# The last expert round taken out of the loop of a mixture-of-experts step, its rows added by a weighted one-hot matmul in PSUM

## What is computed

```python
for g in range(N_GROUPS):                       # 4 groups of 8 experts, top-2 of the best group
    h1 = jnp.einsum('td,edf->tef', xt, exp_w1[g])    # 1024 -> 256
    h3 = jnp.einsum('td,edf->tef', xt, exp_w3[g])
    act = jax.nn.silu(h1) * h3 * comb[:, g, :, None]
    out = out + jnp.einsum('tef,efd->td', act, exp_w2[g])
return x + out.reshape(n, t, D_MODEL)
...
y = rms_norm(x, final_norm_g)
```

## Time and profile before

| | |
|---|---|
| median of 3 runs | 716.58 us (715.87 to 720.83) |
| the profiled execution | 718.26 us, its span 716.3 us |
| PE busy / weight loads | 618.3 us / 451.2 us |
| DVE, ACT, POOL busy | 319.0, 201.5, 79.2 us |
| DMA | 179.38 MB, mean 250 GB/s |
| mean granted clock of PE | 0.931 |

### The profile page before, as it was taken

One profiled execution on the slowest core, in us unless ns is written; L12 is line 12 of the kernel. 1 busy time (PEld: TensorE's weight loads), 2 busy tenths in 40 slices (PEclk: granted clock), 3 DMA queues, 4 the chain that ended last, 5 costly groups with the idle time before them and its releaser, 6 DMA issues.

```text
span 716.3 us, 11504 instructions
## 1 busy us (share of the span) xinstructions
PE 618.3 (86%) x4673; PEld 451.2 (63%) x4673; DVE 319.0 (45%) x629; ACT 201.5 (28%) x343; POOL 79.2 (11%) x129
## 2 busy tenths in 40 slices
PE   4999999989899999999989985999999798398720
PEld 3999998579899999984778862333333343033200
DVE  4748978958544364688413155121121121012038
ACT  5512332254743434436003051121121121012022
POOL 0000000510001210010202111111212111110100
PEclk8999999999999999999989985999999999699965
DMA  9941220324556233669896394899999999999453
GB/s 284 279 141 64 96 82 2 121 79 125 168 129 214 81 118 119 234 239 342 277 389 254 150 350 181 337 420 420 418 421 421 418 422 419 422 420 402 190 233 136
DMA packets 74924, 179.38 MB, mean 250 GB/s; under 512 B 9166, under 2 KB 55946, under 8 KB 61544
## 3 DMA queue, kind: packets, MB, share of 16 engines
q1 hardware_dynamic: 65900, 163.47, 60.9%
q0 software_dynamic: 5600, 12.76, 4.7%
q10 hardware_dynamic: 3372, 2.42, 1.0%
HBM read 172.80 MB, written 15.61 MB: 263 GB/s over the span
## 4 chain that ended last, share of the span: by engine, by line
PE 68%; DMA 17%; DVE 6%; SPq 4%; issue 3%; ACT 2%; ACTq 1%; DVEq 0%; POOLq 0%
DMA w<-exp_w 13%; PE ps L1678 12%; PE ps L1680 12%; PE ps L1679 12%; PE ps L2121 11%; PE ps L2149 4%; PE ps L1827 3%; SPq L612 3%; PE ps L1674 3%; PE ps L1908 2%; DMA raw<-cache_mem_k 2%; DMA xs_rows<-x_sample 1%; PE ps L2008 1%; PE ps L1845 1%; PE ps L1970 1%
## 5 line engine op out<-in xcount | busy, mean ns | idle before, releaser
L2121 PE MATMUL ps<-w,xeT 128*64 128x512 f32 (+2 forms) x512 | 122.9, 652 | 22.9 <-DMA w<-exp_w 21.6
L1678 PE MATMUL ps<-xH,w_h 128*128 128x260 f32 x480 | 139.0, 290 | 0.4 <-DVE xL L1336 0.2
L1679 PE MATMUL ps<-xH,w_l 128*128 128x260 f32 x480 | 136.2, 284 | 0.0
L1680 PE MATMUL ps<-xL,w_h 128*128 128x260 f32 x480 | 136.2, 284 | 0.0
L2121 PEld LDWEIGHTS ps<-w,xeT 128*64 128x64 f32 (+2 forms) x512 | 42.2, 147 | 102.0 <-issue 100.2
L1678 PEld LDWEIGHTS ps<-xH,w_h 128*128 128x128 f32 x480 | 91.1, 190 | 5.6 <-issue 4.9
L1679 PEld LDWEIGHTS ps<-xH,w_l 128*128 128x128 f32 x480 | 91.0, 190 | 0.2
L1680 PEld LDWEIGHTS ps<-xL,w_h 128*128 128x128 f32 x480 | 91.1, 190 | 0.0
L1028 DVE TENSOR_TENSOR w_l<-raw,w_h 128x2048 fp32r<-128x2048 f32 x28 | 64.1, 2289 | 35.5 <-ACT w_h L725 35.5
L2149 PE MATMUL ps<-w,aT 128*64 128x512 f32 (+2 forms) x256 | 58.6, 598 | 9.3 <-DVE aT L1591 9.3
L1584 DVE SCALAR_TENSOR_TENSOR gated<-ps,rs_slot,silu 128x256 f32<-128x256 f32 x14 | 6.8, 483 | 122.3 <-ACT silu L966 122.3
(11 more groups left out here) (364 smaller groups left out, 920.2 us busy)
## 6 DMA issues: line engine op xcount, KB each, us to landing
w<-exp_w SPq DMA_DIRECT2D x96, 1024.0 KB, 21.7
raw<-w_in SPq DMA_DIRECT2D x8, 1024.0 KB, 11.1
raw<-cache_mem_k SPq DMA_DIRECT2D x8, 1024.0 KB, 6.8
raw<-cache_mem_v SPq DMA_DIRECT2D x8, 1024.0 KB, 12.1
raw<-xa_wk SPq DMA_DIRECT2D x4, 1024.0 KB, 5.9
raw<-xa_wv SPq DMA_DIRECT2D x4, 1024.0 KB, 5.7
raw<-xa_wq SPq DMA_DIRECT2D x4, 1024.0 KB, 5.1
raw<-xa_wo SPq DMA_DIRECT2D x4, 1024.0 KB, 5.2
```

What stands on the lines that cost most here:

```text
L1678: pe.matmul(out, h1, h2, start=start, stop=False)
L1679: pe.matmul(out, l1, h2, start=False, stop=False)
L1680: return pe.matmul(out, h1, l2, start=False, stop=stop)
L2121: last = pe.matmul(mm[0][half, j, :], xeT[j][:, k, half], w13[s][:, :, k, :], start=k == 0, stop=k == KT_D - 1)
```

## The change

Round 14 and 15 change their order and their place. The loop now has one round in a turn: places 30 and 31 first (still with the weight slots 0 and 1), then the overflow, two items a turn. Places 28 and 29 (weight slots 2 and 3) become a round of their own, written out after the loop on every engine. Its rows are not scattered. `ye[1]` stays in SBUF, and for each row tile PE adds two products in PSUM: `ident` times `x2` (x with the expert rows that came through `y_rows`), and `back` times `ye[1]`. `back` is a one-hot of slot against token in which the one is the slot's weight. The final norm reads the sum from PSUM.

What goes with that:

- `y_rows` has no entry for the rows of the last round, so SP fills all of it with zeros from `sumsq` early on (after the load numbered 9, during the input projection), 4.26 MB.
- At the end of the routing PE makes each slot's weight with 10 matmuls of one column (`last_w`), DVE brings it to `w_slot` and makes `back` in 5 instructions, and only then raises `route_done`. PE's program has these matmuls ahead of the first `gathered_columns`, which waits for `w_slot` too (`tv_used`). The number of turns is found in 7 chained steps where there were 3.
- Before the loop PE turns the rows of the last round. In the loop PE waits for the scaled columns before `hidden`, and the turn of the next gathered rows comes after `down`.
- In the tail the tiles go in the order `TAIL` = 0, 4, 1, 2, 3. x comes back by tiles on the semaphore of the tile's expert rows; SP reads `y_rows` as soon as the loop's last scatter has landed.
- Nine semaphores of the routing become two (`route_by_pe`, `route_by_dve`), with the same waits. The diff leaves these lines out.

```diff
+                    sp.wait_ge(zero_made, 1)
+                    zeros = sumsq[:, 0:SEQ].rearrange("p (o d) -> p o d", o=1)
+                    sp.dma_start(y_rows[0:8 * P].rearrange("(p a) (h d) -> p (a h) d", p=P, h=2),
+                                 zeros.broadcast_to([P, 16, SEQ])).then_inc(y_zeroed, 16)
+                    sp.dma_start(y_rows[8 * P:2 * T].rearrange("p (h d) -> p h d", h=2),
+                                 zeros[0:2 * NS].broadcast_to([2 * NS, 2, SEQ])).then_inc(y_zeroed, 16)
...
             with sp.Fori(0, loops_n) as it:
-                for r in range(2):
-                    which = [expert_at(it * 4 + (FIXED + 2 * r + n)) for n in range(2)]
-                    rounds = sp.value_load(free_at[0:1, bass.ds(it, 1), r:r + 1].rearrange("p t o -> p (t o)"),
-                                           min_val=1, max_val=PAIRS + 2 * TURNS)
-                    wait(hid_ready, rounds)
-                    for n in range(2):
-                        load_gate_up(2 * r + n, which[n])
-                    wait(y_done, rounds)
-                    for n in range(2):
-                        load_down(2 * r + n, which[n])
+                which = [expert_at(it * 2 + (FIXED + 2 + n)) for n in range(2)]
+                rounds = sp.value_load(free_at[0:1, bass.ds(it, 1)], min_val=1, max_val=PAIRS + TURNS)
+                wait(hid_ready, rounds)
+                for n in range(2):
+                    load_gate_up(n, which[n])
+                wait(y_done, rounds)
+                for n in range(2):
+                    load_down(n, which[n])
+            which = [expert_at(FIXED + n) for n in range(2)]
+            sp.wait_ge(hid_ready, FREE_AT[1])
+            for n in range(2):
+                load_gate_up(2 + n, which[n])
+            sp.wait_ge(y_done, FREE_AT[1])
+            for n in range(2):
+                load_down(2 + n, which[n])
...
             sp.wait_ge(y_done, PAIRS)
-            sp.dma_start(x2[:, 0:4, :], x_rows[0:SEQ].rearrange("(t p) d -> p t d", p=P)).then_inc(x_back, 16)
-            sp.dma_start(x2[0:NS, 4, :], x_rows[SEQ:T]).then_inc(x_back, 16)
+            for t in TAIL:
+                t0, n = TILES[t]
+                sp.dma_start(x2[0:n, t, :], x_rows[t0:t0 + n]).then_inc(yr_in[t], 16)
             sp.dma_start(fin_g[:], a["final_norm_g"].rearrange("(o d) -> o d", o=1).broadcast_to([P, D])).then_inc(fg_in, 16)
-            for j in range(2):
-                wait(y_stored[j], loops_n * 16 + 16 * (PAIRS // 2))
+            wait(y_stored[0], loops_n * 16 + 16 * (PAIRS // 2))
+            sp.wait_ge(y_stored[1], 16 * (PAIRS // 2))
             rows = y_rows.rearrange("(t k) d -> t k d", k=2)
-            for t, (t0, n) in enumerate(TILES):
+            for t in TAIL:
+                t0, n = TILES[t]
                 sp.dma_start(yr[t][0:n], rows[t0:t0 + n]).then_inc(yr_in[t], 16)
...
-            for i in range(1, OVER // 4):
-                link(dve.scalar_tensor_tensor(loops[0:1], total, 4.0 * i, loops[0:1], ALU.is_gt, ALU.add))
+            for i in range(1, OVER // 2):
+                link(dve.scalar_tensor_tensor(loops[0:1], total, 2.0 * i, loops[0:1], ALU.is_gt, ALU.add))
...
             link(dve.reciprocal(wgt[:, 0, :], w_ex[:, 1, :]))
-            dve.tensor_tensor(wgt[:, 1, :], wgt[:, 0, :], w_ex[:, 0, :], ALU.mult).then_inc(route_done, 1)
+            link(dve.tensor_tensor(wgt[:, 1, :], wgt[:, 0, :], w_ex[:, 0, :], ALU.mult))
+            dve.scalar_tensor_tensor(last_hot[:], slot_f[:, 1], float(PAIRS), wgt[:], ALU.is_equal, ALU.mult).then_inc(last_hot_ready, 1)
+            link(dve.tensor_copy(row_f[:], gids[:, PAIRS:PAIRS + 1]))
+            dve.tensor_scalar(row_t[:], tile_no[:], row_f[:, 0:1], -1.0, ALU.subtract, ALU.mult)
+            src = take("last_w")
+            dve.tensor_copy(w_slot[:], src[:, 0:1]).then_inc(tv_used, 1)
+            dve.wait_ge(tv_used, TV_AT["last_w"] + 1)
+            for t in range(NT):
+                last = dve.tensor_scalar(back[:, t, :], count_to[:], row_t[:, t:t + 1], w_slot[:, 0:1], ALU.is_equal, ALU.mult)
+            last.then_inc(route_done, 1)
...
+            columns_right(PAIRS + 1, 1)
...
-                gate_of(it * 2 + PAIRS, 0, rs_now[:, 0:1])
-                columns_right(it * 2 + (PAIRS + 1), 1)
-                act_columns_out(it * 2 + PAIRS)
-                y_right(it * 2 + PAIRS, 0, it * 16 + 16 * (PAIRS // 2))
-                gate_of(it * 2 + (PAIRS + 1), 1, rs_now[:, 1:2])
-                act_columns_out(it * 2 + (PAIRS + 1))
-                y_right(it * 2 + (PAIRS + 1), 1, it * 16 + 16 * (PAIRS // 2))
-                columns_right(it * 2 + (PAIRS + 2), 0)
+                gate_of(it + PAIRS, 0, rs_now[:, 0:1])
+                act_columns_out(it + PAIRS)
+                y_right(it + PAIRS, 0, it * 16 + 16 * (PAIRS // 2))
+                dve.wait_ge(hid_ready, it + (PAIRS + 1))
+                columns_right(it + (PAIRS + 2), 0, False)
+            gate_of(loops_n + PAIRS, 1, rs_slot[:, PAIRS:PAIRS + 1])
+            act_columns_out(loops_n + PAIRS)
+            y_right(loops_n + PAIRS, 1, 16 * (PAIRS // 2))
...
+                dve.wait_ge(yr_in[t], 32)
...
-                dve.scalar_tensor_tensor(yo[t][0:n], x2[0:n, t, :], fin_ss[0:n, t:t + 1], fin_g[0:n],
-                                         ALU.mult, ALU.mult).then_inc(y_out[t], 1)
-
-            add_experts(0)
-            for t, (t0, n) in enumerate(TILES):
-                if t + 1 < NT:
-                    add_experts(t + 1)
-                mean_square(t)
+                dve.scalar_tensor_tensor(yo[t][0:n], in_whole(n_t)[0:n], fin_ss[0:n, t:t + 1], fin_g[0:n],
+                                         ALU.mult, ALU.mult).then_inc(y_out, 1)
+
+            for n_t in range(2):
+                add_experts(TAIL[n_t])
+            dve.wait_ge(fg_in, 16)
+            for n_t in range(NT):
+                if n_t + 2 < NT:
+                    add_experts(TAIL[n_t + 2])
+                mean_square(n_t)
...
+            out = open_tv("last_w")
+            pe.wait_ge(last_hot_ready, 1)
+            for i in range(2):
+                for j, (_, n) in enumerate(TILES):
+                    last = pe.matmul(out[:, 0:1], row_hot[0:n, i, j, :], last_hot[0:n, i, j:j + 1], start=(i, j) == (0, 0),
+                                     stop=(i, j) == (1, NT - 1))
+            last.then_inc(tv_ready, 1)
...
             pe.wait_ge(pass_ready, 1)
-            loops_n = pe.value_load(more[0:1, 0:1], min_val=1, max_val=MORE_ITEMS // 4)
+            pe.wait_ge(xa_ready, PAIRS + 1)
+            pe.wait_ge(xv_ready, PAIRS + 1)
+            gathered_columns(PAIRS + 1, 1, PAIRS // 2 + 1)
+            loops_n = pe.value_load(more[0:1, 0:1], min_val=1, max_val=TURNS)
             with pe.Fori(0, loops_n) as it:
                 slots = [(0, it + 5), (1, it + 5)]
-                hidden(it * 2 + PAIRS, 0, slots)
-                gathered_columns(it * 2 + (PAIRS + 1), 1, it + (PAIRS // 2 + 1))
-                act_columns(it * 2 + PAIRS)
-                down(it * 2 + PAIRS, slots)
-                slots = [(2, it + 5), (3, it + 5)]
-                hidden(it * 2 + (PAIRS + 1), 1, slots)
-                act_columns(it * 2 + (PAIRS + 1))
-                down(it * 2 + (PAIRS + 1), slots)
-                gathered_columns(it * 2 + (PAIRS + 2), 0, it + (PAIRS // 2 + 2))
+                pe.wait_ge(xa_ready, it + (PAIRS + 2))
+                pe.wait_ge(xv_ready, it + (PAIRS + 2))
+                pe.wait_ge(gated_ready, it + PAIRS)
+                hidden(it + PAIRS, 0, slots, False)
+                act_columns(it + PAIRS)
+                down(it + PAIRS, slots)
+                gathered_columns(it + (PAIRS + 2), 0, it + (PAIRS // 2 + 2))
+            pe.wait_ge(xa_ready, loops_n + (PAIRS + 2))
+            pe.wait_ge(xv_ready, loops_n + (PAIRS + 2))
+            slots = [(2, 5), (3, 5)]
+            hidden(loops_n + PAIRS, 1, slots, False)
+            act_columns(loops_n + PAIRS)
+            down(loops_n + PAIRS, slots)
+
+            pe.wait_ge(ya_ready, loops_n + (PAIRS + 1))
+            pe.wait_ge(yv_ready, loops_n + (PAIRS + 1))
+            for n_t, t in enumerate(TAIL):
+                n = TILES[t][1]
+                pe.wait_ge(y_sum, n_t + 1)
+                if n_t == 4:
+                    pe.wait_ge(y_out, 1)
+                for b in range(2):
+                    c = slice(512 * b, 512 * b + 512)
+                    out = in_whole(n_t)[0:n, c]
+                    pe.matmul(out, ident[0:n, 0:n], x2[0:n, t, c], start=True, stop=False)
+                    last = pe.matmul(out, back[:, t, 0:n], ye[1][:, c], start=False, stop=True)
+                last.then_inc(whole, 1)
 
```

174 lines of the change are left out of this document (90 added, 84 removed).

## The result

The changed kernel takes 723.92 us in the median of eight runs (722.14 to 727.21), the kernel before 717.4 in eight (714.93 to 720.83). The ratio is 1.0092 with a 95% interval of 1.0071 to 1.0112: slower by 6.5 us. The forecast was 4.7 us more, within a range of 715.5 to 725.5. The profiled execution took 723.86 us, its span is 722.1.

The account below looks back on a forecast made before the run. Expert weight transfers, opened by round 0, were taken to bound the kernel until round 15, then the tail. +7.7 - 0.5 - 2.5 = +4.7 us on 716.58 gave 721.3 us, with an 8-in-10 range of 715.5 to 725.5.

Parts of the forecast that it names:

- The bound: Expert weight transfers, saturated from 460 us to round 15's start: any delay of round 0 delays the last weights equally.
- Part 1: End of the routing, ahead of round 0: added loops links, narrow matmuls and hand-overs, transposes now behind them; +7.7 us.
- Part 2: Rounds 14 and 15, reordered: last round 1.1 us late, 1.7 us of half clock regained; -0.5 us at last ye.
- Part 3: The tail: scatter and readback behind the last round gone, PE products added; 30.7 us against 33.1, so -2.5 us.
- T: Time of the last ye, from which the prediction counts the tail; forecast end T + 30.7.
- The zeros at nothing: Writing 4.26 MB of zeros during the input projection was to cost 0; 10 us if that cover were gone.
- The front is cheap: Rival: narrow matmuls before round 0 take little or run at 2.4 GHz, +2.8 to +5.0; 717.5 us, chance 0.15.
- the weights have slack: Rival: the front's delay vanishes in the weight transfers and only the tail's gain stands; 713.6 us, chance 0.06.
- The last round comes late: Rival: rounds 14 and 15 lose more, or expert rows land late; +3 to +5, about 725.5 us, chance 0.11.
- Half clock in the tail: Rival: PE's tail products stay at half clock and PE becomes the bound, +11.5 us; 735 us, chance 0.05.
- its point of decision: Sign for the late last round: PE is ready for round 15 later than 671.

Follow-up runs that it names:

- front_alone: Kernel before, plus only last_hot, the ten narrow matmuls and the copy to w_slot, their result unused; measured ratio 1.0086 to the kernel before.
- doubling: Changed kernel, with the 4 MB of zeros written a second time to an array nobody reads; ratio 1.0079 to the kernel before.
- the idle products: Changed kernel, with four unread 512-column products on PE behind the last down product, ahead of the tail; ratio 1.0064 to the kernel before.

## Why the prediction was right, and where it was off

- **The bound.** Right. A delay of round 0 came out at round 12 in full (+7.91, +8.09), in front_alone too (+7.18, +7.57), and taking it away gave it back once nothing else was in the transfers' way.
- **Part 1, +7.7.** Measured +8.1, near the upper end of its range. The terms: the chain of `loops` 1.24 us for 0.51 (forecast 0.68 more), twenty records 4.66 for 4.3, transposes and scaling behind them as counted, and round 0 at half clock for longer, 9.56 us for 9.30. The records were sized by the row of other narrow matmuls at half clock, 0.215 us each, and took 0.233. Twice the full-clock row of one-column records, 2 x 0.118 = 0.236, would have been nearer: those have the same shape. By the rule of the Trainium skill (VectorE: DVE Perf Modes, TRN2 errata) they would take an estimated 1.0 us; this trace disagrees, 4.66 us, of which PE's weight loads were busy 4.61.
- **Part 2, -0.5: the step that failed.** Measured +1.2. Two terms of it were mis-sized. The last round was to start 1.1 us late against the weights and started 2.35 late (10.44 less 8.09). Of this, 1.1 us is a thing that the prediction did not have at all: it took the last round's rows to be there when PE comes for them, and did not follow GpSimd's queue, where their gather stands behind round 12's scatter and then takes 10.38 us. Issued ahead of it, round 14 starts 1.66 us earlier, 0.54 of which its round 12 has already. And of the 1.7 us that the clock was to give back only 1.2 arrived: the last round's hidden values did take 7.09 us for 8.78, but from their end to the turn of `gated` it is 1.59 us for 1.09, so that from the round's start to its `ye` it is 13.40 us for 14.59. Why these 0.5 us were lost stays open.
- **Part 3, -2.5.** Measured -2.39, T + 30.73 for T + 30.7. Not all of it for the right reasons: tile 0's products ended at T + 9.85 and not 8.8, its output at T + 14.0 and not 13.1, which DVE's later turns (0.5) and the last output (3.1 us where 3.4 were counted) took back. The half clock at tile 0 was forecast and there; its price is 2.8 us, not 1.7, as the idle products show. The prediction's end without it, T + 28.8, does not follow from its own terms either: less 1.7 they give T + 29.0, and T + 27.9 was measured.
- **The zeros at nothing.** Right as far as doubling can tell.
- **The rivals.** "The front is cheap" and "the weights have slack" fall. "The last round comes late" was half right: its point of decision, the last round later than 671, is missed by 0.1 us (in the time of the kernel before and less the front's shift it starts at 440.59 + 238.44 - 8.09 = 670.9), and where it had 3 to 5 us over the forecast's term, 1.7 came. The gather that did come late was not among the causes that it lists. "Half clock in the tail" fell as a bound: the stretch ends in tile 0.

The time itself is off by 2.6 us. The three terms make 2.2 of it (front 0.4, last rounds 1.7, tail 0.1), and the median that the forecast started from 0.8 (716.58 of three runs where eight give 717.4); 0.4 goes the other way, since the medians lie 6.5 us apart and the two profiles, from the `band` product on, 6.9.

## What to carry to other kernels

Where a saturated stream sets the end, look for the point that opens it and keep everything off the way to that point: ten matmuls of one column there cost 4.7 us, twice what the tail's rewrite brought (2.4), and the same weights fetched behind round 1, packed, left round 12 within 0.8 us of its place in the kernel before (183.45 and 182.66 for 182.72). When a wait is moved to a round whose data come by an indirect transfer, follow the issuing engine's queue and not only the data. And a transfer of single words takes the DMA engines from the stream beside it: pack them before it goes out. Last, an edit that moves a pause can move a stretch at half clock with it, into the tail or out of it, so read the clock through to the end before putting a gain or a loss down to the edit.
